# Attention mixers of a two-block transformer kernel: where the scores of the later head pairs stand

## What is computed

```
l_own = jnp.einsum('bhqd,bhkd->bhqk', qc, k_own).astype(jnp.float32) * scale + bias_own
probs = jax.nn.softmax(logits, axis=-1).astype(v.dtype)
...
s = jnp.where(mask[None, :, None, None], s, -jnp.inf)
m = jnp.maximum(s.max(-1, keepdims=True), sink)
p = jnp.exp(s - m)
p = p / (p.sum(-1, keepdims=True) + jnp.exp(sink - m))
o = jnp.einsum('bnhgqk,bnkhd->bnqhgd', p.astype(v.dtype), vv)
```

## Time and profile before

| | us |
|---|---|
| median of 3 runs | 901.85 (901.81 to 902.9) |
| the profiled execution, its time | 901.73 |
| its span | 899.9 |
| TensorE busy | 889.7 |
| VectorE busy | 674.3 |
| ScalarE busy | 511.9 |

### The profile page before, as it was taken

How to read it: one execution, slowest core, us unless ns; L and a number is a source line. 1 busy time by engine, 2 the same in 40 slices (tenths; PEclk the granted TensorE clock), 3 DMA queues, 4 the chain that set the end, 5 groups by cost and what they waited for, 6 DMA issues and landing times.

```text
span 899.9 us, 18128 instructions
## 1 busy us (share of the span) xinstructions
PE 889.7 (99%) x6744; PEld 839.1 (93%) x6744; DVE 674.3 (75%) x1114; ACT 511.9 (57%) x764; POOL 120.8 (13%) x78
## 2 busy tenths in 40 slices
PE   8999999999999999999999999999999999999997
PEld 7977999999999999899999999999899999999996
DVE  5975887777777966789766686789777886668665
ACT  7355744334335655977555555567387855555552
POOL 1000000000000023002133230300220122324003
PEclk9999999999999999999999999999999999999999
DMA  8863275565564654436655555444434465565531
GB/s 316 333 226 105 95 245 177 185 197 176 186 192 159 188 187 165 141 118 191 204 180 173 195 180 185 145 141 138 133 113 133 160 212 188 175 197 180 171 138 47
DMA packets 44147, 156.82 MB, mean 174 GB/s; under 512 B 5082, under 2 KB 5573, under 8 KB 43973
## 3 DMA queue, kind: packets, MB, share of 16 engines
q1 hardware_dynamic: 42336, 152.17, 51.4%
q10 hardware_dynamic: 1317, 2.43, 0.7%
q0 software_dynamic: 448, 1.59, 0.6%
HBM read 155.11 MB, written 1.06 MB: 174 GB/s over the span
## 4 chain that ended last, share of the span: by engine, by line
PE 90%; DVE 6%; ACT 2%; issue 1%; DMA 1%; POOL 0%; SPq 0%; DVEq 0%; POOLq 0%; ACTq 0%
PE ps L415 21%; PE ps L416 21%; PE ps L417 21%; PE ps L470 5%; PE ps L472 5%; PE ps L471 5%; DVE w_lo L1445 1%; DVE op_lo L1607 1%; PE ps L558 1%; PE ps L560 1%; PE ps L433 1%; PE ps L559 1%; PE ps L882 1%; PE ps L582 1%; PE ps L440 1%
## 5 line engine op out<-in xcount | busy, mean ns | idle before, releaser
L415 PE MATMUL ps<-op_hi,w_hi 128*128 128x258 f32 (+1 forms) x1330 | 377.2, 284 | 0.2 <-DVE w_lo L1445 0.2
L417 PE MATMUL ps<-op_hi,w_lo 128*128 128x258 f32 (+1 forms) x1330 | 375.0, 282 | 0.0
L416 PE MATMUL ps<-op_lo,w_hi 128*128 128x258 f32 (+1 forms) x1330 | 374.6, 282 | 0.0
L1445 DVE TENSOR_TENSOR w_lo<-raw,w_hi 128x1024 fp32r<-128x1024 f32 x222 | 285.9, 1314 | 22.5 <-ACT w_hi L1055 19.8
L1055 ACT ACTIVATE w_hi<-raw 128x1024 fp32r<-128x1024 f32 x222 | 229.2, 1052 | 67.5 <-PE ps L417 36.2
L415 PEld LDWEIGHTS ps<-op_hi,w_hi 128*128 128x128 f32 x1330 | 251.1, 189 | 3.7 <-DVE w_lo L1445 0.6
L416 PEld LDWEIGHTS ps<-op_lo,w_hi 128*128 128x128 f32 x1330 | 251.8, 189 | 2.1
L417 PEld LDWEIGHTS ps<-op_hi,w_lo 128*128 128x128 f32 x1330 | 250.8, 189 | 0.0
L1048 ACT ACTIVATE w_hi<-raw 128x1024 fp32r<-128x1024 f32 x60 | 63.5, 1058 | 61.7 <-PE ps L417 31.4
L415 PE MATMUL ps<-mix_hi,w_hi 128*128 128x256 f32 x336 | 96.1, 286 | 0.2 <-DVE mix_lo L2068 0.2
L417 PE MATMUL ps<-mix_hi,w_lo 128*128 128x256 f32 x336 | 94.5, 281 | 0.0
(11 more groups left out here) (297 smaller groups left out, 1099.0 us busy)
## 6 DMA issues: line engine op xcount, KB each, us to landing
raw<-in_stream SPq DMA_DIRECT2D x284, 512.0 KB, 3.7
x<-in_x SPq DMA_DIRECT2D x4, 256.0 KB, 5.6
bias<-bias_rows POOLq DMA_DIRECT2D x1, 1024.0 KB, 8.4
work<-in_last_norm SPq DMA_DIRECT2D x1, 1024.0 KB, 5.6
result<-y SPq DMA_DIRECT2D x4, 256.0 KB, 2.0
y<-in_spans ACTq DMA_DIRECT2D x1, 640.0 KB
bias<-bias_rows POOLq DMA_DIRECT2D x1, 512.0 KB, 11.9
proj<-in_gmask ACTq DMA_DIRECT2D x1, 512.0 KB
```

The costliest lines, as they stand in the source:

```text
L415: pe.matmul(o, wh, xh, start=start, stop=False, **kw)
L416: pe.matmul(o, wh, xl, start=False, stop=False, **kw)
L417: return pe.matmul(o, wl, xh, start=False, stop=stop, **kw)
L1445: m = dve.tensor_tensor(w_lo[:, s, :], raw[:, s, :], fp(w_hi[:, s, :]), ALU.subtract)
```

## The change

On TensorE, in three places the scores of a pair no longer stand behind the turning of the pair two before it. They stand behind the values of that pair, with one filler between. In moba these are the scores of pairs 2 and 3, in swa those of the third pair (number 6); the scores of the fourth pair of swa stay. On VectorE and ScalarE the two `pair_attention` are rearranged: on VectorE the shift of the third pair stands behind scale and mix, in moba the shift of the fourth pair too; on ScalarE the split of a unit stands ahead of the exp of the third pair, and in swa the copy of the second pair does too. No instruction is added or removed.

```
@@ -757,14 +757,14 @@
             row_filler(0, 4)
             pe.wait_ge(S["evac"], EV_IN + 14)
             pair_turn(0, 4)
-            moba_scores(2)
             row_filler(1, 4)
             moba_values(0)
+            moba_scores(2)
             row_filler(2, 4)
             pair_turn(1, 5)
-            moba_scores(3)
             row_filler(3, 4)
             moba_values(1)
+            moba_scores(3)
             row_filler(4, 5, 0)
             pair_turn(2, 6)
             row_filler(4, 5, 1)
@@ -824,9 +824,9 @@
             mix_filler(1, 12)
             pe.wait_ge(S["evac"], EV_EVEN + 19)
             pair_turn(4, 12)
-            swa_scores(2)
             mix_filler(2, 12)
             swa_values(0)
+            swa_scores(2)
             mix_filler(3, 12, 0)
             pair_turn(5, 13)
             swa_scores(3)
@@ -1171,9 +1171,13 @@
                 step()
                 pair_exp(g + 1, sink)
                 pair_copy(g)
-                pair_exp(g + 2, sink)
-                step()
-                pair_copy(g + 1)
+                step()
+                if sink:
+                    pair_copy(g + 1)
+                    pair_exp(g + 2, sink)
+                else:
+                    pair_exp(g + 2, sink)
+                    pair_copy(g + 1)
                 pair_exp(g + 3, sink)
                 if sink:
                     step(between=lambda: pair_copy(g + 2))
@@ -1680,13 +1684,16 @@
                 pair_scale(g, sink)
                 pair_shift(g + 1, tile(1), sink)
                 step()
-                pair_shift(g + 2, tile(2), sink)
                 pair_scale(g + 1, sink)
                 pair_mix(g, turned)
-                step()
-                pair_shift(g + 3, tile(3), sink)
+                pair_shift(g + 2, tile(2), sink)
+                step()
+                if sink:
+                    pair_shift(g + 3, tile(3), sink)
                 pair_scale(g + 2, sink)
                 pair_mix(g + 1, turned)
+                if not sink:
+                    pair_shift(g + 3, tile(3), sink)
                 if sink:
                     pair_scale(g + 3, sink)
                 step()
```

## The result

| | us |
|---|---|
| changed kernel, median of 22 runs | 903.24 (902.68 to 903.57) |
| kernel before, median of 22 runs | 901.92 (901.38 to 903.1) |
| ratio | 1.0014, 95% interval 1.0008 to 1.0019 |
| the profiled execution, its time and span | 903.28 and 901.5 |

The change makes the kernel slower by 1.32 us, 0.14%. That is less than the 0.2% which counts as telling in the prediction, but the interval lies above 1, so the loss is real.

The account below looks back on a forecast made before the run. TensorE was taken as the bound everywhere around the change. Moves in moba -0.28, the stall at values 2 +1.66 and swa +0.25 gave +1.63 us on 901.73, so 903.4; range 902.2 to 904.3.

Parts of the forecast that it names:

- The bound: Everywhere around the change: TensorE, busy in 99% of the span; gains come only from shorter gaps between its instructions.
- The worth of a move: On TensorE, turning to filler two on: 5.26 us instead of 5.40, a gain of 0.14 per move without waits.
- x: On TensorE, the way from values into scores, shown by no row: taken as 0.13 us, ends 0 and 0.17.
- The first move: In moba, scores of pair 2 behind values 0: copy 0 in time with 0.28 us to spare, so -0.14.
- the prediction's signs of being wrong: In moba: copy 2 starting before scores 3 plus 5 us, values 0 waiting, or turning 3 showing its own wait.
- The chain from scores 3 to values 2: In moba, through shift, exp, split and copy 2: 6.15 us, so TensorE stands still 1.66 us at values 2.
- What is late next: In moba, turning 3 at 85.86 needs split, scale 3 and mix 2: in time by some 0.8 us.
- swa: Turning 4 to filler 3: values 4 wait 0.58 us for copy 4, filler 3 at 379.52 instead of 379.27, +0.25.
- The sum: Whole kernel: -0.28 + 1.66 + 0.25 = +1.63 us on the profiled 901.73, so 903.4.
- The slower one: Same stall at values 2 in moba, but longer: slower by over 0.2%, 903.6 to 904.4 us; chance 0.32.
- The faster rival: No stall at values 2 in moba, if TensorE starts are only modelled: 901.1 us; chance 0.05.
- The hidden one: Moba's loss taken up by a shrinking wait between mixer and feed-forward: 901.9 to 902.5 us; chance 0.08.

Follow-up runs that it names:

- three splits: The changed kernel with three splits instead of one between exp 3 and copy 2 on ScalarE in moba; 906.69 us, ratio 1.0050.

## Why the prediction was right, step by step

**The bound.** TensorE, as said: every difference above is a wait of TensorE, a way between two of its shapes, or its clock.

**The worth of a move.** Forecast 0.14 for each; measured 0.05 for the first and 0.20 for the second. x, the way from values into scores, was set at 0.13; values to scores is 67.78 - 66.97 = 0.81, exactly the 0.81 that values took into a filler, so x is 0.10. That is also what the rule of the Trainium skill gave ("TensorEngine Tiling (Array Packing)", section "Tiling Modes"): a change of tiling mode drains TensorE, so this way costs like the others. The trace agrees with the size, 0.10; no row shows a drain as such. The estimate by that rule, 0.17 for a move, lies nearer to the 0.20 than mine; the last 0.03 is a filler shorter by that much.

The first move gained less because values 0 waited for copy 0. They came 66.97 - 63.29 = 3.68 behind turning 0, 3.54 in the kernel with the change in moba alone (66.92 - 63.38), where they didn't wait and the same stretch, turning 0 to filler 2, took 68.58 - 63.38 = 5.20. The wait of 0.14 is too short for the profile's list, but copy 0 was at 66.13 and ended at 66.92, just ahead of values 0. A wait of values 0 is one of the prediction's signs of being wrong, and in this one small term it was: I had 0.28 to spare, from one trace, and copy 0 came 2.84 behind turning 0 where it had come 65.80 - 63.46 = 2.34. Exp 1 ahead of the copy was late in the same way, 64.36 - 63.29 = 1.07 behind turning 0 against 64.02 - 63.38 = 0.64 in the kernel with moba alone. This differs between executions, and no cause beyond that was sought.

**The chain from scores 3 to values 2.** Forecast 6.15, measured 81.92 - 75.87 = 6.05. Scores 3 to exp 3 took 2.49, as forecast, exp 1.77 as forecast, the split 0.94 (0.95), the copy 0.79. The rest is the way from the finished copy to TensorE: 0.06 (81.86 to 81.92), not the 0.15 taken from a turning that waited for a mix. The stall came out at 1.56 by the distances, 1.49 in the profile's list, against 1.66 forecast. That it depends on ScalarE's order is shown by taking links out one by one and by adding one and then two. The prediction put the end of mix 1 only 0.09 ahead of scores 3. That holds: a shift that has nothing but the mix ahead of it starts 1.73 behind values 1 (78.00 - 76.27, in the kernel with the queues alone changed), here 1.78, so the scores held it by 0.05. What the prediction didn't draw from this is that the chain would be as late without the moved scores, by VectorE's order.

**What is late next.** Nothing, as said: values 2 to turning 3 is 3.70.

**swa.** Forecast +0.25, measured in the trace +0.14 (5.78 - 5.64) and between medians +0.16, for the change in swa alone. The way from the copy to TensorE was 0.05, not 0.15, and x 0.10, not 0.13. The 0.34 wait at the last turning stayed (0.4), as said. The prediction took the listed 0.2 wait of a step of scores for one in the mixers. It stands at 677.03, but a stall of that size is in swa all the same, unlisted: turning 4 to its scores takes 374.57 - 373.63 = 0.94 before, where turning 0 to its scores takes 0.74. The sum went by distances, so it holds.

**The sum.** Forecast +1.63 against the profiled execution, 903.4. In the traces the mixers lost 1.31 (moba, 1.56 less 0.25) and 0.14 (swa), 1.45 in all; the profiled execution took 1.55 more than that of before, and the medians differ by 1.32, 903.24. What was off in the mixers are sizes: x by 0.03, counted three times, and the way from a copy to TensorE by 0.1, counted twice, made the forecast 0.28 too high; the wait of values 0, 0.14, which it had at nothing, made up for half of that. The rest is a few hundredths in the fillers.

**The rivals.** The slower one needed 0.17 more than forecast and there was less. A price that it hadn't named, the clock, would have carried it: a wait longer by one split cost not 0.95 but 2.56 (+3.88 against +1.32). The faster rival came true only with the copies put ahead; what it leaned on, that TensorE's starts are modelled, isn't so: the profile models the ends. The hidden one fell: the distance from turning 0 to the first transposes of rows behind the mixer grew by 1.31 (94.58 - 63.29, against 93.44 - 63.46), and nothing behind gave it back.

## What to carry to other kernels

When a step is moved later, follow it through every queue that it feeds, not only along its own data: scores 3 belong to pair 3, but what came late was the copy of pair 2, whose data had been there for about 2 us. Ask of a late step also whether it has more than one reason: shift 3 was put behind the scores on TensorE and behind a mix in its own queue, and either was enough. When a producer moves later, move the work that doesn't depend on it ahead of its consumers in the same queues; the same change went from 0.14% slower to no slower that way, and with one more reordering, which has nothing to do with the move, to 0.16% faster. Where TensorE is the bound, gains of a tenth of a microsecond for a way saved are real, but any one short wait eats several of them.

## What was not expected of the hardware

The clock. In the changed kernel TensorE stood for 1.49 us and went on at 2.4 GHz; in the kernel with scores alone moved it stood 2.01 us in moba and did the same. Behind waits of 2.28, 2.44, 2.63 and 3.37 us the granted clock fell from 1.00 to 0.50 (1.2 GHz) for a stretch and then rose again. When it fell differed: while TensorE still stood with 3.37, just after it had taken up its work with 2.44, and about a microsecond later with 2.63 and 2.28. With 2.28 and 2.44 the stretch from values 2 to turning 3 took 5.25 instead of 3.70, so the fall cost 1.55 us on top of the wait; with 2.63 the stretch from scores to values cost 4.01 - 2.46 = 1.55; with 3.37, values 2 to turning 3 took 88.77 - 83.65 = 5.12, 1.42 more. So in these traces a stall of 2.28 us cost 3.8, one of 2.01 no more than itself.

These are single profiled executions, and the fall need not come in every one. Those of the kernel with the queues alone changed range from 904.27 to 906.34, and the two fastest of the five have a mean granted clock of 0.999, the others 0.996 to 0.998. With three splits the fastest, 905.26, has 0.999 and the others 0.996 or 0.997. That fits, but it is not shown: executions of the kernel before, whose profile has no fall in it, range from 0.998 to 1.0 themselves.
